# Reordering one stage of a software pipeline over head pairs: work moved between levels, banks and engines

## The reference

```
def step(S, inp):
    r_t, w_t, k_t, v_t, a_t, b_t = inp
    sa = jnp.einsum('bhij,bhj->bhi', S, a_t)
    S = S * w_t[:, :, None, :] + sa[..., None] * b_t[:, :, None, :] + v_t[..., None] * k_t[:, :, None, :]
    return S, jnp.einsum('bhij,bhj->bhi', S, r_t)
...
y = (_wkv_scan(r4, dec4[0], kd4[0], v4, -kk, kk * a4[0], reverse=False)
     + _wkv_scan(r4, dec4[1], kd4[1], v4, -kk, kk * a4[1], reverse=True))
mean = jnp.mean(y, axis=-1, keepdims=True)
var = jnp.mean(jnp.square(y - mean), axis=-1, keepdims=True)
yn = (y - mean) * lax.rsqrt(var + GN_EPS)
...
o = (yn + bonus).reshape(Bn, T, D).astype(h.dtype) * g
```

## Time and profile before

| what | value |
|---|---|
| three timed runs | 1995.46, 1997.2 (median), 2003.59 us |
| profiled execution | 1991.52 us, span 1989.7 us |
| granted TensorE clock, mean over the span | 0.943 |
| busy share of the span | PE 86%, PEld 68%, DVE 45%, ACT 36%, POOL 31% |
| stages -1 and 0 | 59.9 and 68.1 us |
| stages 1 to 5 together | 348.1 us |
| stage 6 | 60.4 us |

### The profile page before, as it was taken

The page is one execution under the profiler, slowest core; times in us unless marked ns, Lnnn a source line. Parts: engine busy times, 40 slices in busy tenths (PEclk is TensorE's granted clock), DMA queues, the critical chain, the costliest instruction groups (busy, mean ns, idle before and its releaser), DMA issues.

```text
span 1989.7 us, 45604 instructions
## 1 busy us (share of the span) xinstructions
PE 1711.0 (86%) x20212; PEld 1347.5 (68%) x20212; DVE 892.4 (45%) x1135; ACT 716.4 (36%) x1096; POOL 609.7 (31%) x314
## 2 busy tenths in 40 slices
PE   4999668888888888778999999968787699999995
PEld 2777257777777777555777888846565478888884
DVE  3755654465455444444333441045764454444103
ACT  3332233333333332235343332224443354444221
POOL 0432232222232120142333344433111334444443
PEclk8999889999999999889999999989898899999998
DMA  7231000111110100234654233201011123323321
GB/s 298 86 124 32 27 7 8 45 30 30 46 51 9 46 26 5 76 138 190 242 224 177 85 111 102 84 31 59 26 49 37 63 64 95 95 84 109 101 86 42
DMA packets 43883, 161.12 MB, mean 81 GB/s; under 512 B 3664, under 2 KB 18256, under 8 KB 40912
## 3 DMA queue, kind: packets, MB, share of 16 engines
q1 hardware_dynamic: 43728, 158.75, 23.2%
HBM read 156.64 MB, written 2.10 MB: 80 GB/s over the span
## 4 chain that ended last, share of the span: by engine, by line
PE 76%; DVE 13%; ACT 4%; POOL 3%; issue 2%; DMA 1%; ACTq 0%; DVEq 0%; SPq 0%; POOLq 0%
PE ps L531 14%; PE ps L532 14%; PE ps L533 14%; PE ps L794 3%; PE ps L632 2%; PE ps L633 2%; PE ps L634 2%; PE ps L558 2%; PE ps L830 2%; DVE x_res L1551 2%; DVE area L1800 1%; DVE area L1895 1%; PE ps L786 1%; PE ps L812 1%; DVE area L1481 1%
## 5 line engine op out<-in xcount | busy, mean ns | idle before, releaser
L1973 POOL TENSOR_TENSOR split_w<-raw_w,split_w 128x1024 fp32r<-128x1024 f32 (+1 forms) x148 | 380.8, 2573 | 739.2 <-ACT split_w L1135 739.2
L532 PE MATMUL ps<-h_lo_pad,split_w 128*128 128x512 f32 x800 | 320.8, 401 | 0.0
L531 PE MATMUL ps<-h_hi,split_w 128*128 128x512 f32 x704 | 283.0, 402 | 18.4 <-DVE h_lo_pad L1490 18.4
L1135 ACT ACTIVATE split_w<-raw_w 128x1024 fp32r<-128x1024 f32 (+1 forms) x148 | 167.2, 1130 | 354.1 <-PE ps L533 353.9
L533 PE MATMUL ps<-h_hi,split_w 128*128 128x512 f32 x704 | 279.5, 397 | 0.0
L531 PE MATMUL ps<-ff_hi,split_w 128*128 128x512 f32 x448 | 178.7, 399 | 9.0 <-DVE h_lo_pad L1490 9.0
L531 PEld LDWEIGHTS ps<-h_hi,split_w 128*128 128x128 f32 x704 | 133.7, 190 | 69.6 <-issue 29.5
L533 PE MATMUL ps<-ff_hi,split_w 128*128 128x512 f32 x448 | 175.6, 392 | 0.0
L532 PEld LDWEIGHTS ps<-h_lo_pad,split_w 128*128 128x128 f32 x800 | 151.8, 190 | 33.7 <-issue 0.5
L1565 DVE SCALAR_TENSOR_TENSOR ffs<-ffs,fcur 128x512 f32<-128x512 f32 x44 | 82.5, 1876 | 176.5 <-ACT ffs L1168 176.5
L533 PEld LDWEIGHTS ps<-h_hi,split_w 128*128 128x128 f32 x704 | 133.0, 189 | 31.8
(11 more groups left out here) (264 smaller groups left out, 3411.2 us busy)
## 6 DMA issues: line engine op xcount, KB each, us to landing
raw_w<-in_ffn_up SPq DMA_DIRECT2D x88, 512.0 KB, 3.6
raw_w<-in_ffn_down SPq DMA_DIRECT2D x32, 704.0 KB, 4.0
late_a<-in_ada_w SPq DMA_DIRECT2D x7, 2048.0 KB, 8.3
late_b<-in_ada_w SPq DMA_DIRECT2D x7, 2048.0 KB, 9.3
o_res<-in_proj_w SPq DMA_DIRECT2D x24, 512.0 KB, 3.6
area<-in_ada_w SPq DMA_DIRECT2D x12, 1024.0 KB, 6.1
area<-in_ada_w SPq DMA_DIRECT2D x4, 2048.0 KB, 21.3
x_res<-in_xT SPq DMA_DIRECT2D x2, 2048.0 KB, 11.7
```

The lines of the kernel that those rows point to most:

```text
L531: mm(bank, wh[:, o:o + P], hi[:, t], start=(t == 0), stop=False)
L532: mm(bank, wh[:, o:o + P], lo[:, t], start=False, stop=False)
L1135: A(split_w[:, r % 2, 0, 0:cols], raw_w[:, r, 0:cols], ACT.Copy).then_inc(w_hi, 1)
L1973: G.tensor_tensor(split_w[:, r % 2, 1, 0:cols], raw_w[:, r, 0:cols], split_w[:, r % 2, 0, 0:cols].bitcast(F32), ALU.subtract).then_inc(w_l ...
```

## The change

The kernel after does the same arithmetic. What differs is the order and the engine:

- The second direction's identity products move from GpSimd to VectorE, behind its mask, with a semaphore of their own (`ident_back`).
- `select_half` of the pair before and `group_variance` move from behind the first level's system to before it.
- The banks of the rate and decay inputs are swapped, so that the first sigmoid empties bank 1; `solved` waits for that one alone. `lora_decays` moves from behind level 2 into level 3 (counted from 1), and ScalarE's `decays` with it.
- ScalarE loads its tables early: `load_function` runs a one-column activation at the end of the first level (sigmoid), of the third (exponential) and of the fifth (square root).
- VectorE's `rates` move behind the third level's masks, `decays_back` behind the fifth's.
- `bonus_sum` moves from the fourth level to the fifth.
- The first direction's two transposes move from the stage's end to the fifth level, into banks 2 and 3, which the transposed factors no longer need there; ScalarE copies them behind the final factors. The grams in these banks wait for those copies instead.

The core of the diff; lines of the same kind are left out:

```diff
             def first_factors(q):
-                pe.wait_ge(ident_in, 2 * q + 1)
+                pe.wait_ge(ident_in, q + 1)
...
-                pe.wait_ge(ident_in, 2 * q + 2)
+                pe.wait_ge(ident_back, q + 1)
...
             def grams(q):
-                        pe.wait_ge(tev[g - 2], (LEVELS - 1) * (q + 1))
+                        pe.wait_ge(tr_in, 5 * q + g - 1)
...
-            def transposed(q):
-                for g in range(5):
+            def transposed(q, groups):
+                for g in groups:
                     bank = (2, 3, 4, 5, 1)[g]
-                    if g < 4:
+                    if g < 2:
+                        pe.wait_ge(tev[g], (LEVELS - 1) * (q + 1))
+                    elif g < 4:
                         pe.wait_ge(gram_in, 6 * q + 3 + g)
...
   (TensorE, stage)
                     elif l == 1:
                         if scans:
                             if prepares:
-                                pe.wait_ge(evac, 4 * r + 2)
+                                pe.wait_ge(evac, 4 * r + 1)
                             solved(p, 1)
                     elif l == 2:
                         if scans:
                             from_state(p, 2)
+                        if prepares:
+                            lora_decays(r)
                     elif l == 3:
...
-                        if prepares:
-                            bonus_sum(r)
                     else:
                         if scans:
                             solved(p, 3)
+                        if solves:
+                            transposed(q, (0, 1))
+                        if prepares:
+                            bonus_sum(r)
                     if solves:
                         level_factors(q, l)
...
                 if solves:
-                    transposed(q)
+                    transposed(q, (2, 3, 4))
   (ScalarE)
+            def load_function(f):
+                A(warm[:], ct[:, K_EPS:K_EPS + 1], f)
...
   (VectorE, stage)
+                    dve.wait_ge(sys, 2 * q + 2)
+                    own(V.tensor_tensor(nt[:, 1], chunks(ps[:, 3, :]), eight(ct[:, K_NT + C:K_NT + 2 * C]), ALU.mult))
+                    own.wait()
+                    own(V.tensor_tensor(nt[:, 1], nt[:, 1], eight(ct[:, K_EYE:K_EYE + C]), ALU.add))
+                    own.wait()
+                    V.tensor_tensor(xc[:, 1], nt[:, 1], eight(ct[:, K_M1 + C:K_M1 + 2 * C]), ALU.mult).then_inc(ident_back, 1)
```

More of the change, by code:

```diff
@@ L1271, in sigmoid, with rates @@
                 A(dst, ps[:, bank, :], ACT.Sigmoid, bias=pc(col)).then_inc(evac, 1)
-            def rates(r, banks=(7, 1), first=0):
+            def rates(r, banks=(1, 7), first=0):
                 act.wait_ge(pcols, r + 1)
@@ L1279, in rates, with decays @@
                     sigmoid(4 * r + first + n + 1, t_a[n], banks[n], 2 + n)
-            def decays(r, banks=(7, 1), first=2):
+            def decays(r, banks=(1, 7), first=2):
                 act.wait_ge(pcols, r + 1)
@@ L1311, in right_sides, with transposed_out @@
                 A(x0s, ps[:, 0, 0:256].rearrange("p (n q i) -> p n q i", n=NDIR, q=NSEQ), ACT.Copy).then_inc(x0_ev, 1)
+            def transposed_out(q, groups):
+                for g in groups:
+                    act.wait_ge(tr, 5 * q + g + 1)
+                    if g == 0 and q:
+                        act.wait_ge(s_mm, (CPS - 1) * q)
+                    A(kb[:, g // 2, g % 2] if g < 4 else vt, chunks(ps[:, (2, 3, 4, 5, 1)[g], :]), ACT.Copy).then_inc(tr_in, 1)
             def stage(i):
@@ L1336, in stage @@
                         right_sides(p, 2)
+                    if l == 2 and prepares:
+                        decays(r)
                     if solves:
@@ L1368, in stage @@
                     modulation_row(2 * p)
+                if ada_:
+                    modulation_columns(2 * p)
                 if solves:
-                    for g in range(5):
-                        act.wait_ge(tr, 5 * q + g + 1)
-                        A(kb[:, g // 2, g % 2] if g < 4 else vt, chunks(ps[:, (2, 3, 4, 5, 1)[g], :]), ACT.Copy).then_inc(tr_in, 1)
-                        if g == 0 and ada_:
-                            modulation_columns(2 * p)
+                    transposed_out(q, (2, 3, 4))
             decays(0, (2, 3), 0)
@@ L1813, in stage @@
                             finish(b, 2)
+                        if prepares:
+                            rates(r)
                     elif l == 3:
@@ L1824, in stage @@
                         if prepares:
+                            decays_back(r)
                             bonus(r, 1)
@@ L2015, in ident @@
             def ident(q):
[L2017 to L2023 removed]
+                pool.wait_ge(sys_in, q + 1)
+                one = ct[:, K_EYE:K_EYE + C].unsqueeze(1).broadcast_to([P, NCH, C])
+                own(G.tensor_tensor(nt[:, 0], nt[:, 0], one, ALU.add))
+                own.wait()
+                m1 = ct[:, K_M1:K_M1 + C].unsqueeze(1).broadcast_to([P, NCH, C])
+                G.tensor_tensor(mt[:, 0], nt[:, 0], m1, ALU.mult).then_inc(ident_in, 1)
             def keys(r):
```

51 lines of the change are left out of this document (21 added, 30 removed).

## The result

The changed kernel took 1935.4 us (median of four runs, 1933.5 to 1938.0) against 1999.6 for the kernel before on the same chip, a ratio of 0.968 (95% interval 0.9654 to 0.9705). Timed again beside the experiments it took 1940.1 (1935.2 to 1941.6) against 1994.5, ratio 0.9708 (0.9679 to 0.9738). Forecast were 1936, with 1920 to 1962 as range. The profiled execution took 1933.5 (span 1931.7), where 1930 were forecast.

The account below looks back on a forecast made before the run. TensorE's own order and its waits bound the kernel. Savings of 44.6 us (five full stages), 9 (second), 7 (first), 1 and -0.8 (later ones) make 61: 1991.5 profiled becomes 1930, as median 1936; range 1920 to 1962.

Parts of the forecast that it names:

- Stage start: Start of a full stage: TensorE's 1.1 us wait for GpSimd's last identity product goes; VectorE's later work runs about 2 later.
- First level: First level: variance matmul and earlier column selection fill waits of 0.9 and 0.4 us; with the stage's start 0.5 stays.
- Second level: Second level: waiting for one sigmoid and loading the table earlier saves 1.9 us against a wait of 1.6, which goes.
- The second rival: ScalarE's early table load costs twice its 1.28 us and delays the right side: 7 us back, 1943; chance 0.10.
- Third level: Third level: rate operations run behind the masks and decay matmuls fill the gap, so the 1.6 us wait goes.
- Fourth and fifth level: Fourth: bonus matmul and its 0.7 us wait leave. Fifth: transposes and bonus matmul, 3.0 us, cover a gap of 2.8.
- Stage end: End of a stage: 1.92 us of transposes less; last products some 1.2 later, priced at 0, other end 1.3.
- The third rival: Late back decays delay the last products and gram masks at the stage's end: 67 us lost, 2003; chance 0.03.
- The fourth: Rival: filled waits are only handed on to the next engine's latency; about 52 of 61 us return, 1988; chance 0.03.
- Port: Rival: VectorE and GpSimd collide on their shared port, three times a stage reaching TensorE; 27 us back, 1963; chance 0.16.
- Waits that stay or come new: Five full stages: 0.8 us each stays or comes new, leaving 40.6 of the 44.6 us of waits as savings.
- The clock: Five full stages: five of six falls to half clock go, at 0.8 us each, 4 us in all.

Follow-up runs that it names:

- identity_gpsimd: The changed kernel with the identity products of both directions made on GpSimd again; 1942.2 us, ratio 0.973 to the kernel before.
- decays_alone: The kernel before with only VectorE's three back-decay operations moved behind the fifth level's masks and the last solution; 1978.5 us, ratio 0.992.
- both_back: The changed kernel with the transposes at the stage's end and the back decays before the fifth level's masks again; 1966.3 us, ratio 0.984.
- the three parts undone together: The changed kernel with identity products on GpSimd, no early table loads and rate operations before the third level's masks; 1946.2 us, ratio 0.977.
- shift32: The changed kernel with 32 small matmuls more on TensorE behind the first pair's rate matmuls; 1934.3 us, ratio 0.969.

## Why the prediction was right, and where it was not

*What bounds it.* TensorE's order plus the waits inside it: right. All 44.6 us of waits were there to take, and all went.

*Stage start.* The 1.1 went (0.8 of it returns in identity_gpsimd). *First level:* its 0.9 and 0.4 went, with no 0.5 kept; the moves behind that (variance, column selection) had no run of their own.

*Second level.* 1.6 goes, 0.6 by the banks and 1.0 by the early load: the step as worked out. ScalarE in the last full stage after, the last copy, load, one-column activation, right side and the first two sigmoids:
```profile
623.36 0.60 ACT L1366 ACTIVATE area<-ps 128x512 f32<-128x512 f32 x1
623.98 1.28 ACT L1315 ACT_TABLE_LOAD   x1
625.28 0.20 ACT L1315 ACTIVATE warm<-ct 128x1 f32<-128x1 f32 x1
625.39 0.37 ACT L1320 ACTIVATE area<-ps 128x256 f32<-128x256 f32 x1
625.84 1.27 ACT L1276 ACTIVATE h_pad<-ps,pcur 128x512 f32<-128x512 f32 x2
```
The load starts 0.02 behind a copy, takes 1.28 and is followed at once; the 0.20 is the price that was put on the small activation. The second rival, a load that costs double, is out. The drain of about 1.38 that the Trainium skill (ScalarE: Activation LUTs, What ACT_TABLE_LOAD costs) adds to a switch has no room in these rows.

*Third level.* The wait goes, as said; its worth was overrated. Put back, its 7.7 us cost the five stages 0.4 to 1.8 in the one trace taken.

*Fourth and fifth level.* The step "3.0 us of work in a gap of 2.8 [...] a cover that failed would cost it again" is the one that the runs contradict. The 2.8 was the gap with the decays in front of the masks; once they stand behind, it is 0.3 to 1.0 (decays_alone), and the bonus matmul covers that. The transposes fill a gap that is no longer there. VectorE's masks, last solution and back decays in the last full stage after:
```profile
648.13 1.29 DVE L1827 TENSOR_TENSOR area<-ps,ct 128x512 f32<-128x512 f32 x2 [1.17 <-PE ps L773]
649.34 0.41 DVE L1788 COPY area<-ps 128x256 f32<-128x256 f32 x1
649.67 1.64 DVE L1726 TENSOR_TENSOR_SCAN area<-ct,area 128x512 f32<-128x512 f32 x1
...
658.79 0.68 DVE L1756 TENSOR_TENSOR area<-area 128x512 f32<-128x512 f32 x1
660.18 0.69 DVE L1877 TENSOR_TENSOR area<-ps,ct 128x512 f32<-128x512 f32 x1 [0.70 <-PE ps L813]
```
VectorE stood idle 1.17 before the masks: it waits for TensorE now, and not the other way.

*Stage end.* Priced at 0, and right: in that stage the last products end at 659.5, the first gram mask starts at 660.18 behind TensorE's gram. The third rival stays 0.7 short of its point, not the 1.5 to 2 that were given it. The fourth, waits handed on, didn't come as described: no other engine's latency took their place. What came instead is the instruction supply, 11 us of the 52 that it was given.

*Port.* Collisions came where foretold (VectorE's two identity products take 0.93 and 1.64 beside GpSimd's in the last full stage), but in the changed kernel none reached TensorE in the full stages. They did when the decays stood in front of the masks (both_back).

*The terms.* Two were mis-sized, and they offset each other. Waits that stay or come new: 4 in the sum, 13.4 measured in their place (11.2 more than before). The clock: 4 in the sum, while TensorE's busy time fell by 9.5, most of it by the clock. All six falls went, and each had cost 1.2 to 1.5 of its 3.41 us where 0.8 was taken, since TensorE is busy nearly all through a fall (3.07 of 3.41). That is read from the kernel before, where the matmuls of each fall took 8.5 us longer in all than the same ones in the third full stage at full clock. Two rows of it, the fall in the fourth full stage and the same 92 matmuls in the third, columns as in the earlier trace rows:
```profile
640.26:643.67 3.41, 3.41 (x92) 3.41 (x84) 0.20 (x1) 2.39 (x5) 1.17 (x2) 0.50 0.02 5
570.58:572.48 1.90, 1.90 (x92) 1.90 (x86) 0.07 (x1) 1.25 (x3) 0.31 (x1) 1.00 0.04 9
```
So 44.6 was forecast for the five stages and 42.8 measured. That the total came out within 1 us of the forecast is luck to that extent: an error of some 7 us and one of some 5, of opposite sign. The second stage was put at 9 and gave 9.8 (8.1 in the changed kernel timed again); the first at 7 and gave 6.0 (5.0), since VectorE's masks are still late there, 4.7 in place of the earlier trace rows's 9.1, and its gram masks behind them:
```profile
PE ps L787 <- DVE area L1827: 4.7, 3, 2.9
PE ps L817 <- DVE area L1877: 2.7, 1, 2.7
```
What follows the five full stages was put at 0.2 and gave 1.3, within the 3 us by which it varies over the traces.

*What stays open.* Between the kernel before and both_back lie 28 us, yet the three parts undone together cost only 6 by the medians (11 by the ratios) and the fifth level's 26; the rest is in parts that were not run by themselves (variance, column selection, bonus matmul, swapped banks) and in how waits and supply gaps share. In both_back the fifth level's wait did not shrink the supply gaps (13.2), as the third level's did (9.2); why was not tried. Nor was it tried whether the 1 MB transfers delay TensorE's instructions, though both gaps at L759 come within 1 us of the landing of one (491.25 and 554.49, the gaps from 491.8 and 555.4).

## What to carry to other kernels

When a wait can be removed at its source or filled with other work, one of the two may do: here the removal was enough and the filling nearly so. Measure the second with the first in place before you keep it. A fall of the clock cost 1.2 to 1.5 of its 3.41 us here, because the engine was busy all through it. And once an engine's named waits are gone, look for its instruction supply: waits put back may then cost less than their length, because the supply catches up in them (the third level's did, the two shorter ones alone did not).

## What the runs showed of the hardware

TensorE's instructions arrive in blocks. The row of the queue that carries them in the five full stages after:
```profile
q8 instruction: 74, 1.21, 1.6%
```
74 packets of 16 KB for 9425 matmul and 9421 weight rows are 255 instructions each, so an edge every 127 to 128 matmul rows. In the trace of the changed kernel the 25 gaps without a named cause (0.2 us and more, five full stages) all lie on that grid: from one to the next it is 127 to 128 matmul rows or a whole multiple. Each ends 1.2 to 1.6 us behind the end of a packet; the gap of 1.70 that ends at 460.33, for example, follows the packet of 457.62 to 458.77. In shift32 this holds for 24 of 25 gaps. So TensorE waits there for its next block. The packets follow each other at least 3.4 us apart (3.3 in shift32). The 64 rows of L787 and L788, a level's products of both directions, are through in about 1.2 us, the 64 of L795 in 1.86: a block of 128 in 3.1, sooner than the next one follows, and TensorE stands at the edge for 0.2 to 1.7. Two rows of a wide matmul take 1.06 (the variance at 617.26 above); that they give the supply time to catch up is argued from these numbers, not tried.

A scan on VectorE shares the port with GpSimd as the two-operand products of the earlier trace rows do. The first direction's scan in the five full stages after, beside GpSimd's keys (ns, shortest, median, longest):
```profile
L1721 DVE TENSOR_TENSOR_SCAN area<-ct,area x5: 1216/2217/2304, 393.2 to 639.4; 128x512 f32<-128x512 f32 x5
```
Beside GpSimd it takes 2.1 to 2.3. In the stage of the 1.22 it began together with an operation of GpSimd, and that one took 2.29 instead of some 1.3. Alone, the other direction's scan took 1.21 in the kernel before (L1704, all five stages within 1.214 to 1.216).
